# Expert matrices laid on partitions by row, transposes with a step, residual loaded during routing

## The reference, cut to what matters

```python
def expert_block(args):                 # 128 rows of tokens of one expert
    xb, e = args
    hb = jax.nn.silu(xb @ w_gate[e]) * (xb @ w_up[e])
    return hb @ w_down[e]
...
h = rms_norm(x, g_pre_ffn[l]) * (1.0 + sc2) + sh2
y = hier_moe(h, ...)
x = x + gt2 * rms_norm(y, g_post_ffn[l])
```

## Time and profile before

| | us |
|---|---|
| median of 3 runs | 1741.02 (1740.05 to 1744.33) |
| the profiled execution | 1742.48 |
| its span in the trace | 1740.4 |
| mixer | about 0 to 1117 |
| routing | about 1117 to 1165 |
| experts | about 1165 to 1692 |
| combining | about 1692 to 1740 |
| TensorE busy (share of the span) | 1536.9 (88%) |
| DVE busy | 1245.5 (72%) |
| ACT busy | 857.4 (49%) |
| POOL busy | 380.8 (22%) |
| moved by DMA | 291.25 MB |

### The profile page before, as it was taken

How to read it: one execution, slowest core, us unless ns; L and a number is a source line. 1 busy time by engine, 2 the same in 40 slices (tenths; PEclk the granted TensorE clock), 3 DMA queues, 4 the chain that set the end, 5 groups by cost and what they waited for, 6 DMA issues and landing times. The chain is left out here.

```text
span 1740.4 us, 23975 instructions
## 1 busy us (share of the span) xinstructions
PE 1536.9 (88%) x7445; PEld 1164.5 (67%) x7446; DVE 1245.5 (72%) x1981; ACT 857.4 (49%) x1495; POOL 380.8 (22%) x401
## 2 busy tenths in 40 slices
PE   2699987999999999999999999459899999999950
PEld 2589975688946789766889565346576666677630
DVE  4589666469885498965598844486678877877828
ACT  2323262333384423563233523216678778878835
POOL 1000000100001000011000011234366666666630
PEclk9999867999999999999999998659899999999985
DMA  9342334233233332332331323637999998789859
GB/s 330 110 145 97 97 121 170 73 85 97 86 109 98 92 98 89 121 105 78 85 97 50 133 85 97 190 127 231 347 324 316 318 330 253 221 248 315 257 107 361
DMA packets 200421, 291.25 MB, mean 167 GB/s; under 512 B 10559, under 2 KB 158172, under 8 KB 200347
## 3 DMA queue, kind: packets, MB, share of 16 engines
q1 hardware_dynamic: 170720, 197.15, 33.9%
q0 software_dynamic: 29360, 92.99, 19.3%
q10 hardware_dynamic: 266, 0.14, 0.0%
HBM read 240.42 MB, written 59.26 MB: 172 GB/s over the span
## 5 line engine op out<-in xcount | busy, mean ns | idle before, releaser
L930 DVE SCALAR_TENSOR_TENSOR cv<-u,taps,cv 128x512 f32<-128x512 f32 x480 | 321.8, 747 | 0.1
L1757 DVE TENSOR_TENSOR w_rest<-wgu,w_high 128x1024 fp32r<-128x1024 f32 x192 | 233.9, 1223 | 95.1 <-ACT w_high L1682 92.5
L1682 ACT ACTIVATE w_high<-wgu 128x1024 fp32r x192 | 201.4, 1054 | 140.0 <-PE pgu L1632 81.4
L484 PE MATMUL bank<-wo,yT 128*128 128x512 f32 x512 | 227.7, 601 | 2.5 <-ACT hT L660 2.5
L457 PE MATMUL bank<-hT_high,tiles_operand 128*128 128x512 f32 x512 | 201.2, 393 | 9.8 <-DVE hT_operand L903 8.5
L458 PE MATMUL bank<-hT_operand,tiles_operand 128*128 128x512 f32 x512 | 200.3, 391 | 0.0
L459 PE MATMUL bank<-hT_high,win_operand 128*128 128x512 f32 x512 | 200.2, 391 | 0.0
L484 PEld LDWEIGHTS bank<-wo,yT 128*128 128x128 f32 x512 | 97.1, 193 | 118.8 <-issue 118.8
L1642 PE MATMUL py<-wd,hTe 128*128 x384 | 172.6, 592 | 0.9 <-ACT yb L1709 0.9
L1630 PE MATMUL pgu<-w_high,x_high 128*128 128x512 f32 x384 | 155.4, 405 | 0.0
L1631 PE MATMUL pgu<-w_rest,x_high 128*128 128x512 f32 x384 | 151.1, 393 | 0.0
(11 more groups left out here) (330 smaller groups left out, 2873.8 us busy)
## 6 DMA issues: line engine op xcount, KB each, us to landing
win<-w_in_in SPq DMA_DIRECT2D x64, 512.0 KB, 5.1
wgu<-w_gate_in SPq DMA_DIRECT2D x32, 1024.0 KB
wgu<-w_up_in SPq DMA_DIRECT2D x32, 1024.0 KB
wd<-w_down_in SPq DMA_DIRECT2D x32, 1024.0 KB
win<-w_in_in SPq DMA_DIRECT2D x16, 1024.0 KB, 5.1
wo<-w_ada_in POOLq DMA_DIRECT2D x6, 2048.0 KB, 9.8
y_dram<-zeros POOLq DMA_DIRECT2D x17, 512.0 KB, 5.1
tiles<-x_in POOLq DMA_DIRECT2D x16, 512.0 KB, 5.8
```

What stands on the lines that cost most here:

```text
L484: last = nc.tensor.matmul(out[:], yT[:, w % 2, k, :], wo[:, k, half * 512:(half + 1) * 512], start=(k == 0), stop=(k == KD - 1))
L930: ins = V.scalar_tensor_tensor(out=cv[:, j], in0=u[:, j, w:w + T], scalar=tap, in1=cv[:, j], op0=ALU.mult, op1=ALU.add)
L1682: A(w_high[:, QK * q:QK * q + QK, :], c.wgu[:, bass.ds(slot, 1), QK * q:QK * q + QK, :].rearrange("p a k n -> p (a k) n"), ACT.Copy).then_ ...
L1757: V.tensor_tensor(w_rest[:, part, :], c.wgu[:, bass.ds(slot, 1), part, :].rearrange("p a k n -> p (a k) n"), w_high[:, part, :].bitcast(F3 ...
```

## The change

The matrices of the experts go to partitions by row: partition p holds the rows 8p to 8p+7 of gate and up, one run of 8 KB for each, and the rows 2p and 2p+1 of down, one run of 8 KB. Gate and up stand one behind the other in a slot and no longer side by side in each row. So that the products still meet the same features, the transposes take every eighth element of `xg` and every second of `hh`, and the modulation columns are needed in the same order: POOL stores `scale2` and `shift2` to DRAM during routing and loads them back as `scale_by_row` and `shift_by_row`. The eight loads of x1 stand behind the first loads of the experts in the routing stage.

```diff
@@ routing_phase, sync @@
             for e in range(WSLOTS):
                 load_gate_up(sp, ap, c, e, e)
                 load_down(sp, ap, c, e, e)
+            for n in range(NTILES // 2):
+                sp.dma_start(c.x1_all[:, 2 * n:2 * n + 2], ap["x1"][2 * n * P:(2 * n + 2) * P, :]
+                             .rearrange("(t p) n -> p t n", p=P)).then_inc(c.x1_in, 16)
@@ routing_phase, gpsimd @@
+            for n, values in enumerate((c.scale2, c.shift2)):
+                pool.dma_start(ap["mods"][n].rearrange("(k p) -> p k", p=P), values[:], allow_slow_non_contiguous=True).then_inc(mods_stored, 16)
             nc.gpsimd.memset(c.row_weight[:], 0.0)
             nc.gpsimd.memset(c.xg[:].rearrange("p a n -> p (a n)"), 0.0)
+            pool.wait_ge(mods_stored, 32)
+            for n, values in enumerate((c.scale_by_row, c.shift_by_row)):
+                pool.dma_start(values[:], ap["mods"][n].rearrange("(p k) -> p k", p=P)).then_inc(c.by_row_in, 16)
             pool.wait_ge(row_ready, 1)
@@ load_gate_up, load_down @@
-    w = lambda name: ap[name][0][bass.ds(e, 1)].rearrange("a (k p) n -> p (a k) n", p=P)
-    eng.dma_start(c.wgu[:, s, :, 0:FE], w("w_gate")).then_inc(c.gu_in[s], 16)
-    eng.dma_start(c.wgu[:, s, :, FE:2 * FE], w("w_up")).then_inc(c.gu_in[s], 16)
+    for n, name in enumerate(("w_gate", "w_up")):
+        eng.dma_start(c.wgu[:, s, n], ap[name][0][bass.ds(e, 1)].rearrange("a (p k) n -> p (a k) n", p=P)).then_inc(c.gu_in[s], 16)
...
-    eng.dma_start(c.wd[:, s], ap["w_down"][0][bass.ds(e, 1)].rearrange("a (k p) n -> p (a k) n", p=P)).then_inc(c.wd_in[s], 16)
+    eng.dma_start(c.wd[:, s], ap["w_down"][0][bass.ds(e, 1)].rearrange("a (p k) n -> p (a k) n", p=P)).then_inc(c.wd_in[s], 16)
@@ expert_phase @@
+        by_half = lambda w, q: w[:, QK * q:QK * q + QK, :].rearrange("p k (g n) -> p g k n", g=2)
+        loaded = lambda slot, q: c.wgu[:, bass.ds(slot, 1), :, QK * q:QK * q + QK, :].rearrange("p a g k n -> p (a g) k n")
...
-            load_x1(0)
             with sp.Fori(1, ROUNDS) as g:
                 for s in range(WSLOTS):
                     serve(g * WSLOTS + s, s, g + 1)
-                load_x1(g)
...
-                        last = nc.tensor.transpose(pt[half][:, j * P:(j + 1) * P], xg[:, s, k * P:(k + 1) * P], c.ident[:])
+                        last = nc.tensor.transpose(pt[half][:, j * P:(j + 1) * P], xg[:, s].rearrange("p (d k) -> p k d", k=KD)[:, k], c.ident[:])
...
-                    last = nc.tensor.transpose(ph[:, k * P:(k + 1) * P], hh[:, k * P:(k + 1) * P], c.ident[:])
+                    last = nc.tensor.transpose(ph[:, k * P:(k + 1) * P], hh[:].rearrange("p (d k) -> p k d", k=FE // P)[:, k], c.ident[:])
...
-                A(w_high[:, QK * q:QK * q + QK, :], c.wgu[:, bass.ds(slot, 1), QK * q:QK * q + QK, :].rearrange("p a k n -> p (a k) n"),
-                  ACT.Copy).then_inc(w_high_ready, 1)
+                A(by_half(w_high, q), loaded(slot, q), ACT.Copy).then_inc(w_high_ready, 1)
...
+            act.wait_ge(c.by_row_in, 32)
             e, slot = rank_of(act, 0)
...
-                V.tensor_tensor(w_rest[:, part, :], c.wgu[:, bass.ds(slot, 1), part, :].rearrange("p a k n -> p (a k) n"),
-                                w_high[:, part, :].bitcast(F32), ALU.subtract).then_inc(w_rest_ready, 1)
+                V.tensor_tensor(by_half(w_rest, q), loaded(slot, q), by_half(w_high, q).bitcast(F32), ALU.subtract).then_inc(w_rest_ready, 1)
...
             dve.sem_inc(w_rest_ready, 1)
+            dve.wait_ge(c.by_row_in, 32)
@@ build @@
+        ap["mods"] = nc.dram_tensor("mods_dram", (2, D), F32, kind="Internal").ap()
...
-            c.wgu = eb("wgu", [P, WSLOTS, KD, 2 * FE])
+            c.wgu = eb("wgu", [P, WSLOTS, 2, KD, FE])
```

More of the change, by code:

```diff
@@ L1241, in routing_phase @@
         hot_ready, rank_ready, onehot_used = sem("hot_ready"), sem("rank_ready"), sem("onehot_used")
+        mods_stored = sem("mods_stored")
         spread_ready, ranks_ready = sem("spread_ready"), sem("ranks_ready")
@@ L1516, in next_down @@
                 load_down(sp, ap, c, e, s)
-            def load_x1(n):
-                sp.dma_start(c.x1_all[:, bass.ds(2 * n, 2)], ap["x1"][bass.ds(2 * n * P, 2 * P), :]
-                             .rearrange("(t p) n -> p t n", p=P)).then_inc(c.x1_in, 16)
             def gate_up_landed(r, s, turn):
@@ L1690, in empty_turned @@
                 for k in range(4):
-                    last = A(x_raw[:, k, :], pt[0][:, k * P:(k + 1) * P], ACT.Identity, scale=c.scale2[:, k:k + 1], bias=c.shift2[:, k:k + 1])
+                    last = A(x_raw[:, k, :], pt[0][:, k * P:(k + 1) * P], ACT.Identity, scale=c.scale_by_row[:, k:k + 1], bias=c.shift_by_row[:, k:k + 1])
                 last.then_inc(x_raw_act, 1)
@@ L1755, in rest_of_weights @@
                 dve.wait_ge(w_high_ready, 4 * b + q + 1)
-                part = slice(QK * q, QK * q + QK)
-                V.tensor_tensor(w_rest[:, part, :], c.wgu[:, bass.ds(slot, 1), part, :].rearrange("p a k n -> p (a k) n"),
-                                w_high[:, part, :].bitcast(F32), ALU.subtract).then_inc(w_rest_ready, 1)
+                V.tensor_tensor(by_half(w_rest, q), loaded(slot, q), by_half(w_high, q).bitcast(F32), ALU.subtract).then_inc(w_rest_ready, 1)
             def empty_turned(b):
@@ L1765, in empty_turned @@
                     k = 4 + j
-                    last = V.tensor_scalar(x_raw[:, k, :], pt[1][:, j * P:(j + 1) * P], c.scale2[:, k:k + 1], c.shift2[:, k:k + 1], ALU.mult, ALU.add)
+                    last = V.tensor_scalar(x_raw[:, k, :], pt[1][:, j * P:(j + 1) * P], c.scale_by_row[:, k:k + 1], c.shift_by_row[:, k:k + 1], ALU.mult, ALU.add)
                 last.then_inc(x_raw_dve, 1)
@@ L1924, in build @@
             c.rounds = eb("rounds", [P, 1], I32)
-            c.wgu = eb("wgu", [P, WSLOTS, KD, 2 * FE])
+            c.wgu = eb("wgu", [P, WSLOTS, 2, KD, FE])
+            c.scale_by_row, c.shift_by_row = eb("scale_by_row", [P, KD]), eb("shift_by_row", [P, KD])
+            c.by_row_in = c.sem("by_row_in")
             c.wd = eb("wd", [P, WSLOTS, FE // P, D])
```

## The result

| | before | changed |
|---|---|---|
| median of 8 runs each, one beside the other, us | 1740.94 (1737.98 to 1745.75) | 1750.15 (1745.51 to 1758.44) |
| the profiled execution, us | 1742.48 | 1749.91 |
| its span | 1740.4 | 1747.8 |
| mixer | 1116.9 | 1115.2 |
| routing | 48.4 | 50.2 |

The ratio is 1.0052, with a 95% interval of 1.0028 to 1.0075: slower, by 5 to 13 us. The forecast had the sign and 2.6 times the size (+24 us instead of +9.2), and the rows show that its reason isn't there. The mixer's own time varies by more than the routing's difference from one execution to the next (1106.0 to 1117.3 us in the traces of this study, with the same code), so the stages are compared one by one.

A forecast was written before the change was run, and what follows sets the result against it. TensorE was taken as the bound, at 10.00 us per block in the experts' stage. Strided transposes +35 us and recovered loading -11 gave +24 on 1741.0, so 1765 us, range 1730 to 1782.

The forecast's parts named there:

- What bounds the kernel: Experts' stage: TensorE, busy 99.67 of 100 us, sets 10.00 us per block; ACT and DVE have about 1.7 us to spare.
- The failed step: Transposes of xg: each stepped load on TensorE costs 0.10 us more, 35 us in all.
- Rival 1: Transposes: TensorE hides the stride, blocks stay at 10.00 us and 9 us come back, 1732 us; chance 0.31.
- The sign that loads of hidden rows stay unchanged: In the changed kernel's timeline, TensorE's loads for the hidden rows' transposes would be as before.
- The recovery: Experts' stage: better weight loading returns 11 us of the 11.6 us lost, bounds 9 to 11.
- Longer runs: Gate and up loads in 8 KB runs: several us more per full 100 us stretch; no loss expected.
- Modulation columns: POOL's stores and loads during routing: POOL free at about 1130 us, 15 us in time; cost 0.
- Rival 3: Routing: modulation columns come late behind the full DMA queue, 10 us on top of the forecast, 1775 us; chance 0.03.
- ACT's and DVE's split reads: Splitting of weights in runs of 256 elements costs 0; a tenth more, 0.4 us per block, fits the spare time.
- the start: First gathers of the experts' stage overlapping the early loads: taken as 0, bounds 0 and +3 us.
- the hidden rows' steps: Two transposes of hidden rows per block with a step of 8 bytes: taken as 0, up to 11 us.
- Rival 4: Experts' stage: transfers return nothing, gaps come from elsewhere; 1776 us with the strided price, 1741 without; chance 0.08.

The follow-up runs named there:

- e1: Kernel before with only the eight residual loads moved behind the first weight loads in routing: 1725.97 us, ratio 0.9925.
- e11: Kernel before with only the residual loads moved, measured a second time: 1729.95 us, ratio 0.9943.
- e2: Changed kernel with the residual loads put back among the expert loads, so the new layout alone: 1750.79 us, ratio 1.0077 to the kernel before.
- e3: Changed kernel with gate and up in pieces of 1 KB in SBUF, down as before: 1735.42 us, ratio 0.9987 to the kernel before.
- e4: Changed kernel with gate and up in pieces of 4 KB in SBUF, down as before: 1735.60 us, ratio 0.9986 to the kernel before.

## Why the prediction was wrong

**What bounds the kernel** held: TensorE's order, 10.00 us per block, with DVE and ACT slack beside it. It left out one party. POOL, with 65.51 of 100 us busy in the earlier trace rows, I took for idle; with its waits its round was already as long as a block from about 1320 us on, and the five small waits for gathers in the earlier trace rows were the sign.

**The failed step** is "0.72 ns more per element ... so 44 x 8 x 0.10 = 35 us". It carried VectorE's price for a step of 32 bytes over to TensorE's loads. Measured: 0.05 us per block, 2.4 us in all. Each load is 0.05 us longer, but consecutive ones overlap, and eight take 0.98 us instead of 0.91. Rival 1 had this right and was given 0.31; its own argument against itself, that the loads stand nose to tail and nothing is left to hide behind, was the mistake. The Trainium skill (Advanced Engine Details and Errata, "SBUF Cachelines") would make a step of 8 bytes free and one of 32 not; the rows show 197 and 194 ns, the same for both, so on TensorE the measurement decides against it. The sign that loads of hidden rows stay unchanged failed with it (144 to 197 ns).

**The recovery** of 11 us was right in size: hidden-row waits fell by 6.6 us and the half-clock stretches are put at 3.5, 10.1 us together, and e1 and e11 show 10 to 13 us by ratio for the residual alone. That the bounds reached from 6.2 to 11.6 was sound. The two sources don't add, as e2 shows; and ACT still waited once, 4.6 us, where the forecast had no such wait.

**Longer runs: "Nothing speaks for a loss"** was the second error, and it decided. POOL's gathers and scatters land later beside longer pieces, and I never priced them: +14.8 us of waits. With that term at 0, the step at 2.4 us and routing's 1.9 us the sum would have been 1741.0 + 2.4 - 11 + 1.9, about 1734. e3 and e4, which have short pieces, come out at 1739 us on the same scale (0.9987 and 0.9986 of 1741.0), so some 4 us are still not accounted for.

**Modulation columns** (cost 0): the path was right, POOL was free at 1133.5 instead of 1130 us. The cost lay elsewhere, in VectorE's hold, 1.9 us; the 1.83 us of the cast before would have shown it to whoever compared it with its neighbour's 0.23. Rival 3's fear of late columns was half true (14 us to land), inside the slack.

**ACT's and DVE's split reads and the start** cost nothing that can be seen, as forecast; the hidden rows' steps are within the 0.05 us per block. DMA was busy until about 1169 us, not 1165. **Rival 4** fell with e1.

So the sign came out right by luck, through a wait that none of the cases had: forecast +35 - 11; read from the traces, +2.4 + 14.8 - 6.6 - 3.5 in the experts (the last by difference) and +1.9 in routing.

## What to carry to other kernels

Before a large stream gets longer pieces, look at who else uses the DMA engines with a short deadline; a small wait for a gather (2.1 us in 300) says that this deadline is already met only just. A price per element belongs to the engine on which it was read. And a change of two parts wants each part measured alone: here the residual loads moved into an idle stretch, with the old layout kept, give 0.6 to 0.75% (e11 and e1), the best version found, and the new layout takes that back and more.

## What the runs showed of the hardware

- A load of a stationary operand of 128x128 f32 for a transpose lasts 0.144 to 0.148 us side by side and 0.194 to 0.197 with a step of 8 or of 32 bytes; eight in a row take 0.91 and 0.98 us. Loads without a step beside products with 512 columns last 0.189 us too.
- A gather of another queue that TensorE had to wait for was there 5.5 to 7.1 us after the end of its issue beside a stream in pieces of 1 KB (gate and up) and 4 KB (down), once 7.9; beside one in pieces of 8 KB 7.4 to 8.9 us, once 9.7. The stream alone moves 352 to 380 and 419 to 426 GB/s.
- While 2048 stores of 4 bytes were under way, a stream that moved 376 and 352 GB/s without them moved 42 GB/s over 5 us and 120 over the next 5; the stores took 14 us to land.
- A cast of 128x128 on VectorE takes 0.23 us alone, 1.83 beside POOL's clearing of 128x2048 and 3.68 beside two stores and this clearing.
